# Output rows of the experts stored by GpSimd instead of ScalarE, and their weights in a ring of ten matrices

## The reference: what is computed

```python
xb = uf[buf_tok].reshape(n_blocks, MOE_BLOCK, D)
def expert_block(args):
    xblk, e = args
    h = jax.nn.silu(xblk @ w_gate[e]) * (xblk @ w_up[e])
    return h @ w_down[e]
yb = lax.map(expert_block, (xb, block_e)).reshape(P, D)
y = jax.ops.segment_sum(yb * buf_w[:, None].astype(yb.dtype), buf_tok, num_segments=N)
```

## Time and profile before

| | before |
|---|---|
| median of 3 runs | 1954.38 us (1954.33 to 1954.8) |
| the profiled execution, whole | 1960.13 us |
| its span, first to last instruction | 1958.3 us |
| PE busy | 1670.5 us, 85% of the span |
| DMA: moved, mean rate | 333.54 MB, 170 GB/s |
| expert loop, first gathered rows to last store | about 1221 to 1902 us |

### The profile page before, as it was taken

One profiled execution on the slowest core, in us unless ns is written; L12 is line 12 of the kernel. 1 busy time (PEld: TensorE's weight loads), 2 busy tenths in 40 slices (PEclk: granted clock), 3 DMA queues, 4 the chain that ended last, 5 costly groups with the idle time before them and its releaser, 6 DMA issues.

```text
span 1958.3 us, 37977 instructions
## 1 busy us (share of the span) xinstructions
PE 1670.5 (85%) x14820; PEld 1248.8 (64%) x14820; DVE 714.4 (36%) x1304; ACT 484.8 (25%) x879; POOL 429.4 (22%) x376
## 2 busy tenths in 40 slices
PE   2889999999776999999998980998899879999970
PEld 1768777777554787777886870656656656656550
DVE  1534444445678334445225653111111111111118
ACT  1433333334645112001003100112121211121214
POOL 3312222121113333233321203111111111111112
PEclk7889999999887999999999975999999999999995
DMA  9101110100601433442115129399999999849726
GB/s 293 44 22 43 33 42 21 42 22 14 215 1 33 126 100 98 118 155 75 48 64 164 44 100 356 132 410 366 344 352 342 359 342 348 346 187 404 315 65 230
DMA packets 177650, 333.54 MB, mean 170 GB/s; under 512 B 27782, under 2 KB 102414, under 8 KB 177558
## 3 DMA queue, kind: packets, MB, share of 16 engines
q1 hardware_dynamic: 145774, 272.59, 38.5%
q10 hardware_dynamic: 21656, 29.64, 4.7%
q0 software_dynamic: 10128, 29.95, 4.4%
HBM read 302.44 MB, written 29.72 MB: 170 GB/s over the span
## 4 chain that ended last, share of the span: by engine, by line
PE 51%; DMA 27%; DVE 10%; ACT 3%; issue 2%; POOL 1%; SPq 1%; ACTq 0%; DVEq 0%; POOLq 0%
DMA d_y<-yb 23%; PE ps L708 23%; PE ps L868 6%; PE ps L893 5%; PE ps L938 4%; PE ps L784 3%; PE ps L750 3%; PE ps L948 2%; DMA w_exp<-in_w_exp_up 2%; DMA ada_g<-in_ada_w 1%; PE ps L775 1%; PE ps L834 1%; PE ps L900 1%; DVE br_lo L1416 1%; DVE br_hi L1417 1%
## 5 line engine op out<-in xcount | busy, mean ns | idle before, releaser
L938 PE MATMUL ps<-w_exp,xT 128*32 128x256 f32 x6272 | 359.8, 381 | 9.0 <-DMA w_exp<-in_w_exp_up 8.9
L708 PE MATMUL ps<-u_hi,w_hi 128*128 128x512 f32 x768 | 315.8, 411 | 16.7 <-POOL w_lo L541 16.3
L938 PEld LDWEIGHTS ps<-w_exp,xT 128*32 128x32 f32 x6272 | 254.6, 111 | 97.1 <-issue 13.0
L708 PE MATMUL ps<-u_lo,w_hi 128*128 128x512 f32 x768 | 303.5, 395 | 0.0
L708 PE MATMUL ps<-u_hi,w_lo 128*128 128x512 f32 x768 | 303.3, 395 | 0.0
L1589 DVE TENSOR_TENSOR act<-act,ps 64x256 f32<-64x256 f32 x98 | 41.6, 425 | 504.6 <-ACT act L1184 503.1
L948 PE MATMUL ps<-w_exp,actT 128*32 128x256 f32 x3136 | 204.7, 404 | 0.0
L708 PEld LDWEIGHTS ps<-u_hi,w_hi 128*128 128x128 f32 x768 | 146.6, 191 | 50.1 <-issue 24.3
L540 POOL CAST w_hi<-w_raw 128x1024 fp32r<-128x1024 f32 x48 | 54.1, 1128 | 540.4 <-PE ps L708 456.1
L708 PEld LDWEIGHTS ps<-u_hi,w_lo 128*128 128x128 f32 x768 | 146.1, 190 | 31.9
L633 POOL DMA_INDIRECT xg<-d_u,tok_cur x100 | 96.0, 960 | 311.7 <-PE ps L923 295.9
(11 more groups left out here) (255 smaller groups left out, 2192.8 us busy)
## 6 DMA issues: line engine op xcount, KB each, us to landing
w_exp<-in_w_exp_gate SPq DMA_DIRECT2D x32, 2048.0 KB
w_exp<-in_w_exp_up SPq DMA_DIRECT2D x32, 2048.0 KB
w_exp<-in_w_exp_down SPq DMA_DIRECT2D x32, 2048.0 KB
ada_g<-in_ada_w ACTq DMA_DIRECT2D x32, 512.0 KB, 3.8
d_y<-yb ACTq DMA_DIRECT2D x98, 128.0 KB
w_raw<-in_w_in SPq DMA_DIRECT2D x24, 512.0 KB, 4.1
w_raw<-in_w_branch_gate SPq DMA_DIRECT2D x24, 512.0 KB, 4.0
ada<-in_ada_w SPq DMA_DIRECT2D x4, 2048.0 KB, 15.3
```

Source lines behind the costliest of these rows:

```text
L708: ins = pe.matmul(ps[:, 5 + h, :], a[par][:, kc, :], b[:, kc, HF[h]], start=(n == 1), stop=(n == MM))
L938: last = pe.matmul(ps[CAP * n:CAP * (n + 1), 2 + h, 0:QT], x, w_exp[:, sl, off:off + QT], start=(kc == 0), stop=(kc == KC - 1))
```

## The change

Two things change.

1. The two stores of a turn move from ScalarE's stream to the end of GpSimd's turn, behind the two gathers. ScalarE still copies PSUM to `yb[h]`. The zeroing of the spare rows of `d_y` becomes two transfers that count on the same semaphores as the stores.
2. `w_exp` becomes ten buffers of one matrix (the tenth lies at 176 KB, where the routing's scratch was). Matrix m = 3i + (0, 1, 2 for gate, up, down) goes to buffer m mod 10, once matrix m - 10 has been used. SyncE reads all `starts` ahead of the loop, and loads `gffn`, `gffn_b` and `fing` (whose places overlap the tenth buffer) behind the last weights.

```diff
-            def load_expert(i, w):
-                sl = slot_at(i)
-                dst = w_exp[:, sl, part_of[w]:part_of[w] + KC * FE].rearrange("p (q n) -> p q n", q=4)
-                sp.dma_start(dst, exp_v[w][expert_at(i)]).then_inc(ld_wt[w][sl], 16)
+                r, _ = matrix_at(i, w)
+                sp.dma_start(w_exp[r][:].rearrange("p (q n) -> p q n", q=4), exp_v[w][expert_at(i)]).then_inc(ld_wt[r], 16)
...
+            used = [None] + [sp.value_load(starts[0:1, i + 1:i + 2], min_val=i + 2, max_val=NPAIR + 1) for i in range(NE)]
+            def wait_used(m):
+
+                sp.wait_ge(y_ps[1] if m % 3 == 2 else gu_ps[1], used[m // 3 + 1])
+
+            for m in range(RING - 1, 3 * NE):
+                if m >= RING:
+                    wait_used(m - RING)
+                load_expert(m // 3, "gud"[m % 3])
+            wait_used(3 * (NE - 2) - 1)
...
-            for i in range(SLOTS, NE):
-
-                used = sp.value_load(starts[0:1, i - 2:i - 1], min_val=2, max_val=NPAIR + 1)
-                sp.wait_ge(gu_ps[1], used)
-                for w in "gu":
-                    load_expert(i, w)
-                sp.wait_ge(y_ps[1], used)
-                load_expert(i, "d")
...
                     pool.wait_ge(xg_ps, p * 2 + h)
                     hold(pool)
                     gather_rows(h)
+                for h in range(2):
+                    pool.wait_ge(y_evac, p * 2 + (h + 2))
+                    hold(pool)
+                    rows = d_y[bass.ds(p * PAIR - PAIR + h * CAP, CAP), :].rearrange("t (n m) -> n t m", n=4)
+                    pool.dma_start(rows, yb[h][:]).then_inc(st_y[h], 16)
...
                 sc.activation(yb[h][:], ps[:, 6 + h, 0:QT], ACT.Copy).then_inc(y_evac, 1)
-                sc.wait_ge(y_evac, p * 2 + (h + 2))
-                hold(sc)
-                rows = d_y[bass.ds(p * PAIR - PAIR + h * CAP, CAP), :].rearrange("t (n m) -> n t m", n=4)
-                sc.dma_start(rows, yb[h][:]).then_inc(st_y[h], 16)
```

More of the change, by code:

```diff
@@ L31 @@
 LIST = 2 * NPAIR + 2
-SLOTS = 3
+RING = 10
 QT = D // 4
@@ L79, in expert_at, with matrix_at @@
     return EPG * group_at(i % NG) + i // NG
-def slot_at(i):
-    return SLOTS - 1 - i % SLOTS
+def matrix_at(i, w):
+    m = 3 * i + "gud".index(w)
+    return m % RING, 16 * (m // RING + 1)
 def band(r):
@@ L186, in build @@
         wr = at("wr", 202, [P, KC, NE])
-        w_exp = at("w_exp", 32, [P, SLOTS, 3 * KC * FE])
+        w_exp = [at(f"w_exp{r}", kb, [P, KC * FE]) for r, kb in enumerate((128, 144, 160, 80, 96, 112, 32, 48, 64, 176))]
         xg = [at(f"xg{h}", 192 + h, [P, QT]) for h in range(2)]
@@ L306, in build @@
             "ld_rt", "score_ready", "hit_ready", "rank_ps", "slots_ready", "starts_ready", "st_list", "ld_list", "tok_ready"))
-        zero_set, st_pad = sem("zero_set"), sem("st_pad")
-        ld_wt = {w: [sem(f"e_ld_{w}{i}") for i in range(SLOTS)] for w in "gud"}
+        zero_set = sem("zero_set")
+        ld_wt = [sem(f"e_ld{r}") for r in range(RING)]
         quarter_ready, tok_ready4 = sem("e_quarter"), sem("e_tok4")
@@ L584, in _ @@
             pool.wait_ge(zero_set, 1)
-            spare = NPAIR - NE
-            pool.dma_start(d_y[NE * PAIR:, :].rearrange("(p k) (a n) -> p (k a) n", p=P, n=2 * P),
-                           zero_row[:].unsqueeze(1).to_broadcast([P, spare * PAIR * D // P // (2 * P), 2 * P])).then_inc(st_pad, 16)
+            spare = (NPAIR - NE) // 2 * PAIR
+            for h in range(2):
+                rows = d_y[NE * PAIR + spare * h:NE * PAIR + spare * (h + 1), :].rearrange("(p k) (a n) -> p (k a) n", p=P, n=2 * P)
+                pool.dma_start(rows, zero_row[:].unsqueeze(1).to_broadcast([P, spare * D // P // (2 * P), 2 * P])).then_inc(st_y[h], 16)
             pool.wait_ge(gelu_ready, 1)
@@ L930, in hidden_to_features, with gate_up @@
                 last.then_inc(ht_ps, 1)
-            def gate_up(h, sl):
+            def gate_up(h, i):
+                w = [w_exp[matrix_at(i, n)[0]] for n in "gu"]
                 for kc in range(KC):
@@ L936, in gate_up, with down @@
                     for n in range(4):
-                        off = part_of["gu"[n // 2]] + kc * FE + QT * (n % 2)
-                        last = pe.matmul(ps[CAP * n:CAP * (n + 1), 2 + h, 0:QT], x, w_exp[:, sl, off:off + QT],
+                        off = kc * FE + QT * (n % 2)
+                        last = pe.matmul(ps[CAP * n:CAP * (n + 1), 2 + h, 0:QT], x, w[n // 2][:, off:off + QT],
                                          start=(kc == 0), stop=(kc == KC - 1))
                 last.then_inc(gu_ps[h], 1)
-            def down(h, sl):
+            def down(h, i):
+                w = w_exp[matrix_at(i, "d")[0]]
                 for fc in range(FC):
@@ L946, in down @@
                     for n in range(4):
-                        off = part_of["d"] + fc * D + QT * n
-                        last = pe.matmul(ps[CAP * n:CAP * (n + 1), 6 + h, 0:QT], a, w_exp[:, sl, off:off + QT], start=(fc == 0), stop=(fc == FC - 1))
+                        off = fc * D + QT * n
+                        last = pe.matmul(ps[CAP * n:CAP * (n + 1), 6 + h, 0:QT], a, w[:, off:off + QT], start=(fc == 0), stop=(fc == FC - 1))
                 last.then_inc(y_ps[h], 1)
@@ L962, in _ @@
                         pe.wait_ge(xT_ready, p * 2 + h)
-                        gate_up(h, sl)
+                        gate_up(h, i)
                     pe.wait_ge(act_ready, p * 2)
@@ L977, in _ @@
                         pe.wait_ge(y_evac, p * 2 + h)
-                        down(h, sl)
+                        down(h, i)
         @block.scalar
@@ L983, in _ @@
             ch = Chain(sc, ch_act)
-            for s_, n_ in ((p_ready, PRIME), (pt_ready, PRIME), (y_ready, PRIME), (silu_ready, 1), (y_evac, 3), (st_y[0], 16), (st_y[1], 16), (mrow_ready, 1), (st_mod, 16)):
+            for s_, n_ in ((p_ready, PRIME), (pt_ready, PRIME), (y_ready, PRIME), (silu_ready, 1), (y_evac, 3), (mrow_ready, 1), (st_mod, 16)):
                 sc.sem_inc(s_, n_)
@@ L1105, in _ @@
             sc.wait_ge(f_done, 4)
-            sc.wait_ge(st_pad, 16)
+            for h in range(2):
+                sc.wait_ge(st_y[h], 16)
             for b in range(3):
```

12 lines of the change are left out of this document (5 added, 7 removed).

## The result

The changed kernel takes **2036.9 us** (median of 4 runs, 2031.27 to 2040.02), the kernel before 1954.36 (4 runs) beside it: a ratio of 1.042 (95% interval 1.040 to 1.045), 82.5 us slower. The forecast was 2000 within 1915 to 2070, slower with 78%.

A forecast was written before the change was run, and what follows sets the result against it. The prediction took ScalarE's stores of about 13 us, on four DMA engines, to bound the loop. 29 turns of 15.8 and 19 of 12.5 give 696 us against 657.5, +38, with the clock +45: 2000 us, range 1915 to 2070.

The forecast's parts named there:

- likeliest case: Whole kernel: late gathers outweigh the freed stores, 2000 us, own range 1965 to 2050; chance 65%.
- Stores leave ScalarE: Expert loop: with stores on GpSimd a turn can fall from 13.70 towards 12.27 us, at most 69 us gained.
- Gathers move behind the stores: GpSimd's turn: gathers wait for both stores; turns last 12.5 us with idle queues, 15.8 us behind weights.
- The landing among weights: Gathers behind streaming weights: time from issue to landing, 6.0 us, bounds 5.2 to 7.3.
- 29 late turns: Expert loop: the first turn of experts 1 to 29 has its gathers behind weights, 29 of 48 turns at 15.8 us.
- The clock term: TensorE in late turns: granted clock drops after waits, 0.25 us a late turn, 7 us in all.
- The delay part: Expert loop without the clock: 29 turns of 15.8 and 19 of 12.5 us, 696 us against 657.5, +38.
- The ring: nothing: Weight buffers: one matrix more of prefetch costed at nothing, as TensorE hardly waited for weights before.
- the gather lands in time: Rival, expert loop: gathers land sooner than 6.0 us even among weights, at most 17 late turns, 1897 to 1943 us; 17%.
- gather held up in its own queue: Rival, GpSimd's queue: slow stores hold gathers up, turns behind weights 18.9 us, +128, 2083 us; 13%.
- four engines stay the bound: Rival, stores: they stay on the same four engines whoever issues them, turns stay 13.7 us, 1954 us; 5%.
- the third rival: No change: stores stay bound by the same four engines, turns stay at 13.7 us, 1954 us; 5%.

The follow-up runs named there:

- scalar_split4: The kernel before, with each ScalarE store cut by partitions into four of 32 rows; 1907.96 us, ratio 0.976.
- kept_busy_24: The changed kernel with 24 unread matmuls a turn laid into TensorE's wait for the gathered rows; 2042.73 us, ratio 1.044.
- gathers_ahead: The changed kernel with GpSimd's loop turned by one step, so the next gathers are issued before this turn's stores; 1890.87 us, ratio 0.967.
- store0_first: The changed kernel with GpSimd storing half 0, then issuing the next two gathers, then storing half 1; 1951.42 us, ratio 0.997.

## Why the prediction came out as it did

The way was right: gathers behind the stores, landings too late behind streaming weights, as many late turns as forecast. The size was 83 us for 46, and half or more of the loop's loss came through the clock, which the forecast had at 7 us. That the time still fell inside the range is in part luck: the clock's price lay outside its own bounds, and too much delay made up for some of it. (By its own terms, +15 and +105, the likeliest case's range is 1969 to 2059 and not 1965 to 2050.)

- **"Stores leave ScalarE"**: right. The store is gone from the chain, ScalarE's copy waits for `down` alone, quiet turns are 12.0 us (forecast 12.5). `scalar_split4` shows that the reading behind it, four engines, holds.
- **"Gathers move behind the stores"**: right in place. Of the terms up to the gathers' issue two were off. The copy of half 1 ends 0.6 us after `gate_up` starts and not 1.24: the forecast read it from a turn in which ScalarE still issued a store between its two copies. And the store's issue on GpSimd takes 0.74 us, where the forecast said no less than 1.27. So gather 1 goes out at 4.5 and not 5.7 us.
- **The landing among weights**: forecast 6.0, from 5.2 to 7.3. By the example turn half 1's rows, issued at 1554.27, were transposed from 1560.9: some 6.6; over the 28 late turns it is 6.9 in the mean. Median over all gathers 6.4, quiet ones with them, largest 8.2; 6.0 and 7.3 in the earlier trace rows. The early issue and the late landing nearly cancel: transposes at 11.4 us where 11.7 was said.
- **29 late turns**: 28, and the first turn of an expert each time, as was said.
- **The clock term**: this is the step that failed. "I take 0.25 us a late turn, between nothing and 1 us each": it is 2.1 us, 59 us and not 7. The forecast took the price from one stretch of the kernel before after a wait of 7 us, and spread it thin, as if such a drop were rare. In the changed kernel it comes in every one of the 28 late turns. `kept_busy_24` shows that idle time of TensorE is its cause. Nor did the forecast see that the 657.5 us, against which it set turns without a slow clock, hold some 19 us of it already (estimate above). The delay part alone was overestimated: 678 us for the loop against the 696 forecast.
- **"The ring: nothing"**: right within 0.2%, even where the loop runs at 400 GB/s.
- **The rival "the gather lands in time"** (17%): out. It needed at most 17 late turns, and landings did not get shorter without the pile-up on four engines: 6.4 us in the median.
- **The rival "gather held up in its own queue"** (13%): out. `gathers_ahead` has the same queue and the fastest loop. What neighbours cost there is some 0.6 us of a gather's landing.
- **The rival "four engines stay the bound"** (5%): out; in the late turn above, with weights and stores in flight, the share is 1.02. In steps of 1 us with weights in flight, a share near 0.26 (0.18 to 0.36) comes 45 times in the loop before, often several in a row, and 11 times in the changed one, never two in a row.

How a store of the same pattern came to land soon enough on GpSimd's queue can be read from the packet counts. The kernel before moves (21656 - 8720) / 98 = 132.0 packets a store through ScalarE's queue, that is 128 pieces and 4 more; the changed kernel 144.0 through GpSimd's (24256 - 10128 = 14128, less 16 for the second zeroing, by 98), 128 and 16 more; the cut store (27536 - 8720) / 392 = 48.0, 32 and 16 more. The rows of the queues on the page of the kernel before and on the changed kernel's:

```profile
q10 hardware_dynamic: 21656, 29.64, 4.7%
q0 software_dynamic: 10128, 29.95, 4.4%
```

```profile
q0 software_dynamic: 24256, 42.96, 6.5%
q10 hardware_dynamic: 8720, 16.80, 2.7%
```

The Trainium skill (DMA: Bandwidth & Descriptors, Why a DMA increments its semaphore by 16 and not by 1) says that a transfer from SP or ACT is completed by only the engines that carry it, always the lowest-numbered ones, while one from GpSimd is completed by all 16 and, when it is carried by fewer, by consecutive ones that move on from transfer to transfer. By that rule the 4 and 16 extra packets agree, and stores on GpSimd no longer pile up on the same four engines; that the four move on is not shown by any row here, only that no four fell behind. The same page (Issuing engines are not separate DMA queues) says that who issues matters for little but issue time; the third rival followed it. Here it did matter: issued by ScalarE the store bound the loop, issued by GpSimd no copy waited for it. The measurement decides.

## What to carry to other kernels

When an instruction moves behind another on an in-order engine, look not at what the pair costs but at which releaser the ones behind now wait for. Here the next turn's gathers came to stand behind the turn's last copy; the same stores behind them instead made a loss of 4.2% a gain of 3.3%. Price idle time of TensorE together with what follows it at half clock, turn by turn, where the trace of such turns shows the clock falling, and look first how much of that the old time already holds. And a store that takes long although the engines are not busy is worth a look at its outermost dimension.

## What was unexpected of the hardware

- After a wait of about 3 us in a late turn the granted clock was 0.50 for the start of `down`: 5.94 us for 64 matmuls that take 3.66. A gather that starts 1.6 us and lands 0.7 us sooner (`store0_first` against the changed kernel) moved the kernel by 85 us, some 53 of them this way (estimate: half of TensorE's busy time at 0.50, 131 us against 24; 28 such `down` against 7).
- A store issued by GpSimd keeps the engine for 0.74 us, less than a gather's 1.0 us, and the same pattern that took 13 us from ScalarE among streaming weights was never waited for from GpSimd.
- With a quarter of the DMA engines' time free (share 0.74 over the changed kernel's loop), the order of four issues on one engine decided: 281 GB/s there, 350 with the gathers ahead.
